# Two fused projection stages: the last SwiGLU part taken chunk by chunk, the first silu between the norm's steps, the first weight block in halves

## The reference, cut to what matters

```python
xp = xp + ab_out(...) @ w_out             # output projection and residual add
h = rmsnorm(x, norm_ffn[layer])
x = x + (silu(h @ w_gate) * (h @ w_up)) @ w_down      # D_FF = 2816
# layer 0 only, at the head of layer 1:
h = rmsnorm(x, norm_mix[1]);  z = h @ w_qkv           # 1024 x 3072
```

## Time and profile before

| | us |
|---|---|
| median of three runs | 3500.93 (3499.95 to 3503.22) |
| the profiled execution | 3503.33 |
| its span, first to last instruction | 3501.2 |
| PE busy in it | 3178.9 (91%) |
| trunk0, first load to last product | 903.2 to 2114.4 |
| trunk1, first load to last product | 2563.5 to 3471.7 |

### The profile page before, as it was taken

One profiled execution on the slowest core, in us unless ns is written; L12 is line 12 of the kernel. 1 busy time (PEld: TensorE's weight loads), 2 busy tenths in 40 slices (PEclk: granted clock), 3 DMA queues, 4 the chain that ended last, 5 costly groups with the idle time before them and its releaser, 6 DMA issues. The chain is left out here.

```text
span 3501.2 us, 48490 instructions
## 1 busy us (share of the span) xinstructions
PE 3178.9 (91%) x19094; PEld 3024.3 (86%) x19094; DVE 1108.2 (32%) x2190; ACT 846.2 (24%) x1606; POOL 993.7 (28%) x656
## 2 busy tenths in 40 slices
PE   6997558699889999999989996999978999999998
PEld 5997337588889999999989995777778999999997
DVE  3111672445131221112232113665623122112223
ACT  3001333355231111111131002444423111111111
POOL 3211102101352222223252213445435232222320
PEclk8998768799999999999999997999989999999998
DMA  3222514822211111111102225443421111111101
GB/s 107 99 92 75 141 48 142 86 58 62 73 49 37 36 60 48 36 36 60 36 25 74 95 73 128 91 95 82 84 73 48 37 36 60 48 36 36 60 12 58
DMA packets 201725, 230.20 MB, mean 66 GB/s; under 512 B 62400, under 2 KB 177297, under 8 KB 201377
## 3 DMA queue, kind: packets, MB, share of 16 engines
q1 hardware_dynamic: 201600, 228.51, 23.3%
HBM read 181.92 MB, written 54.44 MB: 68 GB/s over the span
## 5 line engine op out<-in xcount | busy, mean ns | idle before, releaser
L1101 PE MATMUL trunk_banks<-hhi,trunk_whi 128*128 128x384 f32 (+1 forms) x3072 | 1007.2, 328 | 58.6 <-POOL trunk_wlo L1044 34.3
L1103 PE MATMUL trunk_banks<-hhi,trunk_wlo 128*128 128x384 f32 (+1 forms) x3072 | 1004.5, 327 | 0.0
L1102 PE MATMUL trunk_banks<-hlo,trunk_whi 128*128 128x384 f32 (+1 forms) x3072 | 1004.5, 327 | 0.0
L1101 PEld LDWEIGHTS trunk_banks<-hhi,trunk_whi 128*128 128x128 f32 x3072 | 579.6, 189 | 60.4 <-POOL trunk_wlo L1044 34.7
L1102 PEld LDWEIGHTS trunk_banks<-hlo,trunk_whi 128*128 128x128 f32 x3072 | 579.6, 189 | 0.8
L1103 PEld LDWEIGHTS trunk_banks<-hhi,trunk_wlo 128*128 128x128 f32 x3072 | 579.5, 189 | 0.0
L1044 POOL TENSOR_TENSOR trunk_wlo<-trunk_stage,trunk_whi 128x2048 fp32r<-128x2048 f32 x86 | 395.7, 4614 | 552.8 <-ACT trunk_whi L980 552.8
L1171 DVE TENSOR_TENSOR trunk_act<-trunk_silu,trunk_banks 128x384 f32<-128x384 f32 x132 | 70.0, 532 | 970.5 <-PE trunk_banks L1103 947.4
L1178 DVE TENSOR_TENSOR xT<-xT,trunk_banks 128x384 f32<-128x384 f32 (+1 forms) x528 | 280.5, 532 | 235.5 <-PE trunk_banks L238 235.4
L1050 POOL TENSOR_TENSOR trunk_alo<-trunk_act,trunk_ahi 128x384 fp32r<-128x384 f32 x132 | 128.0, 970 | 793.8 <-ACT trunk_ahi L993 793.8
L236 PE MATMUL trunk_banks<-trunk_ahi,trunk_whi 128*128 128x384 f32 (+1 forms) x1056 | 346.3, 328 | 3.8 <-DVE xT L1178 3.8
(11 more groups left out here) (306 smaller groups left out, 4109.9 us busy)
## 6 DMA issues: line engine op xcount, KB each, us to landing
trunk_stage<-in_w_gate SPq DMA_DIRECT2D x22, 1024.0 KB
trunk_stage<-in_w_up SPq DMA_DIRECT2D x22, 1024.0 KB, 5.2
trunk_stage<-in_w_down SPq DMA_DIRECT2D x22, 1024.0 KB, 4.8
trunk_stage<-in_w_qkv SPq DMA_DIRECT2D x12, 1024.0 KB, 5.2
park_z<-in_rows SPq DMA_DIRECT2D x22, 544.0 KB
in_stage<-in_w_in SPq DMA_DIRECT2D x11, 1024.0 KB
park_z<-trunk_stage SPq DMA_DIRECT2D x48, 192.0 KB, 1.9
band_q_in<-park_z SPq DMA_DIRECT2D x32, 272.0 KB
```

Of the source, the lines that this page charges most:

```text
L1101: nc.tensor.matmul(out, tiles_of(m, whi)[:, f, k, :], hhi[:, k, c0:c0 + w], start=(k == 0), stop=False)
L1102: nc.tensor.matmul(out, tiles_of(m, whi)[:, f, k, :], hlo[:, k, c0:c0 + w], start=False, stop=False)
L1103: last = nc.tensor.matmul(out, tiles_of(m, wlo)[:, f, k, :], hhi[:, k, c0:c0 + w], start=False, stop=(k == KT - 1))
```

## The change

- **First block in halves.** The first `w_out` block is loaded as two DMAs of 512 KB, each into a contiguous half of 128 columns; ACT copies each half, and DVE instead of POOL subtracts it. The other blocks are as before.
- **First silu among the norm's steps.** ACT takes the silu of (c0, half 0) between `high` of c1 and `root` of c2, and that of (c0, half 1) behind `high` of c2; DVE's two products move along. The split of the first `w_down` block comes behind them, on ACT and on POOL.
- **Last part of trunk0 chunk by chunk.** PE does gate and up of c0 and c1, down of c0, gate and up of c2, down of c1, down of c2, then `w_qkv`. Down products rotate over three banks (4 to 6), bank 7 holds `means` and `roots` of the norm ahead, and its scratch `hf` moves to `stage[2]`; the `w_qkv` products use banks 0 to 3 and leave through `silu` and `act32`. The low parts of the first two `w_qkv` blocks are made on DVE (`low_of`), among the adds, instead of on POOL.

The diff, cut to its core (the rest splits functions by chunk without moving a step):

```diff
 # FlowNorm.total, with shared=True for the norm ahead
-        if c >= 2:
-            pe.wait_ge(self.eps_added, c - 1)
+        n = len(self.means)
+        if c >= n:
+            pe.wait_ge(*((self.scaled, KT * c) if self.shared else (self.eps_added, c - n + 1)))
...
 # SP
-            for u in range(3):
+            for h in range(2):
+                sp.dma_start(halves_of(stage[2])[:, h], columns(w_out)[:, :, h * P:(h + 1) * P]).then_inc(first_in[h], 16)
+            for u in (1, 2):
                 load_columns(A_SET[u], columns(w_out), u)
...
 # ACT
+            for h in range(2):
+                act.wait_ge(first_in[h], 16)
+                nc.scalar.activation(halves_of(whi[2])[:, h], halves_of(stage[2])[:, h], ACT.Copy).then_inc(first_hi, 1)
...
             norm.high(act, 1)
+            silu_of(0, 0, 0, first=True)
             norm.root(act, 2)
             norm.high(act, 2)
-            split(2, 2, a_sum, 24)
-            hidden(0, first=True)
+            silu_of(0, 0, 1, first=True)
+            for f in range(F):
+                high_of(0, 0, f)
+            split(2, 1, a_sum, 24)
+            for c in range(1, NC):
+                hidden(0, c)
...
+                for n in range(KT):
+                    ahead.square(act, n, added, O * LAST + n + 1)
+                silu_of(LAST, 2, 0)
+                ahead.root(act, 0)
+                ahead.high(act, 0)
+                silu_of(LAST, 2, 1)
...
 # POOL, last part
-                for u in range(2):
-                    split(u, 1 + parts)
-                for n in range(2 * KT):
+                for n in range(KT):
                     ahead.keep(pool, n)
                 ahead.low(pool, 0)
-                for n in range(2 * KT, O):
+                hidden(LAST, 2)
+                for n in range(KT, O):
                     ahead.keep(pool, n)
...
 # PE, last part
+                gate_up(LAST, 0)
+                gate_up(LAST, 1)
+                pe.wait_ge(w_lo[2], LAST + 2)
+                down_of(LAST, 0, last=True)
+                gate_up(LAST, 2)
+                down_of(LAST, 1, last=True)
+                down_of(LAST, 2, last=True)
...
 # DVE
+            def low_of(u):
+                dve.wait_ge(w_hi[u], 2 + parts)
+                nc.vector.tensor_tensor(wlo[u][:], stage[u][:], whi[u][:], ALU.subtract).then_inc(w_lo[u], 1)
```

More of the change, by code:

```diff
@@ L910, in trunk_stage @@
         stored = [st.sem(f"stored{r}") for r in range(BANKS)]
+        first_in = [st.sem(f"first_in{h}") for h in range(2)]
+        first_hi, first_lo = st.sem("first_hi"), st.sem("first_lo")
+        rows = [x[:, f, :] for x in (silu, act32) for f in range(F)]
         quarter = lambda tile, i: tile[:, i * W:(i + 1) * W]
@@ L1068, in _ @@
             norm.low(pool, 2)
-            split(2, 2)
-            hidden(0)
+            hidden(0, 0)
+            split(2, 1)
+            for c in range(1, NC):
+                hidden(0, c)
             with pool.Fori(1, LAST) as i:
@@ L1104, in product_of, with gate_up @@
                 return last
-            def part(i, first=False, last=False):
+            def gate_up(i, c, first=False):
+                w = CHUNKS[c][1]
+                for f in range(F):
+                    n = G * i + c * F + f
+                    if not (first and c == 0):
+                        pe.wait_ge(product, n - 1)
+                    for m, done in ((0, gate_sum), (1, up_sum)):
+                        if first and c == 0:
+                            pe.wait_ge(a_added, len(A_ORDER) - BANKS + 2 * f + m + 1)
+                        product_of(banks[:, 2 * f + m, 0:w], m, f, c, norm if first and f == m == 0 else None).then_inc(done, 1)
+                    if first and c == 0 and f == 0:
+                        norm.total(pe, 2)
+                    if i is LAST and ahead and c == 2 and f == 0:
+                        ahead.total(pe, 0)
@@ new lines, in down_of @@
+            def down_of(i, c, first=False, last=False):
+                c0, w = CHUNKS[c]
+                down = [t[2][:].rearrange("p (f k n) -> p k f n", f=F, k=KT) for t in (whi, wlo)]
+                pe.wait_ge(act_lo, G * i + (c + 1) * F)
+                for k in range(KT):
+                    d, b = c * KT + k, 4 + k % 4
+                    if last:
+                        b = 4 + d % 3
+                        pe.wait_ge(added, O * i + d - 2 if d >= 3 else O * i)
+                    elif not (first and d < BANKS):
+                        pe.wait_ge(added, O * i + d + 1 - BANKS)
+                    three_pass(nc, banks[:, b, 0:w], down[0][:, k], down[1][:, k], ahi, alo, F, c0, w).then_inc(out_sum, 1)
+                    if last and d == 2 * KT + 5:
+                        ahead.total(pe, 1)
@@ L1107, in part, with weights @@
+            def weights(i):
                 for m in range(2):
                     pe.wait_ge(w_lo[m], i + 2)
-                for c, (c0, w) in enumerate(CHUNKS):
-                    for f in range(F):
-                        n = G * i + c * F + f
-                        if not (first and c == 0):
-                            pe.wait_ge(product, n - 1)
-                        for m, done in ((0, gate_sum), (1, up_sum)):
-                            if first and c == 0:
-                                pe.wait_ge(a_added, len(A_ORDER) - BANKS + 2 * f + m + 1)
-                            product_of(banks[:, 2 * f + m, 0:w], m, f, c, norm if first and f == m == 0 else None).then_inc(done, 1)
-                        if first and c == 0 and f == 0:
-                            norm.total(pe, 2)
@@ L1120, in part @@
-                pe.wait_ge(w_lo[2], i + 3)
-                down = [t[2][:].rearrange("p (f k n) -> p k f n", f=F, k=KT) for t in (whi, wlo)]
-                for c, (c0, w) in enumerate(CHUNKS):
-                    pe.wait_ge(act_lo, G * i + (c + 1) * F)
-                    for k in range(KT):
-                        if not (first and c == 0 and k < BANKS):
-                            pe.wait_ge(added, O * i + c * KT + k + 1 - BANKS)
-                        three_pass(nc, banks[:, 4 + k % 4, 0:w], down[0][:, k], down[1][:, k], ahi, alo, F, c0, w).then_inc(out_sum, 1)
-                        if last and ahead and c and k == 3:
-                            ahead.total(pe, c - 1)
@@ L1202, in _ @@
             with dve.Fori(1, LAST) as i:
-                gated(i)
+                for c in range(NC):
+                    for f in range(F):
+                        gated(i, c, f)
                 for c in range(NC):
```

225 lines of the change are left out of this document (144 added, 81 removed).

## The result

The changed kernel takes 3453.49 us (median of four runs, 3447.62 to 3454.34) against 3502.07 before; the ratio is 0.985 with a 95% interval of 0.9824 to 0.9876. The forecast was 3452, so the time and all three terms of the sum came out near what was written. The profiled execution of the changed kernel took 3453.55, its span is 3451.8.

The account below looks back on a forecast made before the run. PE, busy 91% of the span, was taken as the bound, so its waits and slow stretches counted. Gains 10.8 + 29.4 + 9 = 49.2 from 3500.93 gave 3451.7, say 3452 us; range 3445 to 3461.

Parts of the forecast that it names:

- The halves: Head of both stages: first w_out block in halves cuts issue to first product to 7.0 us, gaining 10.8 in all.
- the bounds of 4.0 and 6.0: Head gain per stage: 4.0 us if the half lands at 5.84, 6.0 if it lands in 3.9 flat.
- Two signs that the prediction named: Head: a half load landing after 5 us or more meant wrong; heads the same in both stages meant right.
- The first silu: Part 0, both stages: moving the silu early removes the 12 us waits and slow stretches behind them, gaining 29.4 us.
- The page's rule against this edit: Part 0: 1283 ns table load plus some 1380 ns drain per change of set; some 2 us less gain.
- The end of trunk0: Last part of trunk0, chunk by chunk: new waits of 6.6 us against 16.8 lost before; gain taken as 9.
- the discount from 10.2 to 9: End of trunk0: gain lowered because the four short waits may cost some time at the lower clock level.
- the 16.8 of the sum: Old end of trunk0: time lost in 41.58 us, of which 12.0 idle and 4.8 at the lower level.
- the second silu was not late: Rival, part 0: scale and high of c2 drag over 2.4 us; 10 us less gain, 3462; chance 5%.
- no wait moved elsewhere: Rival: waits only move, to w_down or the second block; time stays near 3500; chance 2%.
- the clock stood at 1.00 through the 271 us: Rival, w_qkv phase: short waits bring the clock to 1.2 GHz and it stays; beyond 3590 us; chance 2%.
- The first rival: End of trunk0 gives nothing: waits grow from 6.6 to 16.8 us, total gain 40, time 3461; chance 7%.

Follow-up runs that it names:

- the added copies: Changed kernel with unused 2048-column copies ahead of ACT's second silu in part 0: two in trunk0, three in trunk1 (3460.17 us), or five and one (3458.89 us).
- the kernel with the end spaced out: Changed kernel with adds, low_of, second weight copy and emptying of first w_qkv banks reordered at the end of trunk0: 3447.35 us, ratio 0.9851 to before.

## Why the prediction was right

- **What bounds the kernel.** PE's waits and the stretches behind them were taken as the whole account, and they were: 49.9 us by the marks against 49.2 written. The waits in the two stages went from 70.5 to 30.1 us, and what was lost behind them at the lower level, by the granted clock, from 14.0 to 3.8: 40.4 and 10.2 less. Each of these marks is from one profile and scatters by about 1 us; means over all profiles that share a part give 9.8 for the heads, 28.6 for part 0 and 10.2 for the end, 48.6 in all.
- **The halves: 10.8 written, 10.2 measured** (9.5 in the run with the halves alone). In trunk0 the chain is 4.52 + 1.06 + 1.23 with 0.08 of handoffs, as written; copy and subtraction took the same in every profile with halves. The mis-sized term is the load: 4.5 us to ACT's copy was taken, and it was 5.71 in trunk1, so that the head gives 4.7 there, inside the bounds of 4.0 and 6.0. (With 7.0 for the new head, the 12.78 of the earlier trace rows would have given 5.8 in trunk1 and not the 5.4 of the sum.) That trunk0 came out as written is luck: over the sixteen heads with a half load in the runs it took 4.05 to 5.73 us, 5.1 in the mean, and only one was shorter than this 4.52. Two signs that the prediction named went against it here, a half load of 5 us or more and two heads that are not the same (they differ by 1.2). The mechanism stands, and the size of this term was off.
- **The first silu: 29.4 written, 30.2 measured** (29.6 alone). The steps came as written: `high` of c1 to the gated product 2.39 us (2.4), slack 5.1 (5.2) and 2.3 (2.4) by the trace, 2.6 by the added copies. The slow stretch behind the wait went with it. Of the 30.2, 1.0 is not the silu's: the stretch at the lower level behind the two heads, which this mark holds as well, happened to be that much shorter (0.67 to 0.74 and 0.54 to 0.63 over 6 us).
- **The page's rule against this edit.** The trace has 1.28 for the load, and a silu 1.30 and 1.29 us after its load began, in an order that now loads three times. The Trainium skill, page "ScalarE: Activation LUTs", section "What ACT_TABLE_LOAD costs", adds some 1380 ns of drain to each change of set; the trace does not agree, since no such time stands on either side of a load here, and two such drains, 2.8 us as an estimate from that page's figure, would have used up the slack of 2.3.
- **The end of trunk0: 9 written, 9.5 measured.** The four waits were priced at 2.8, 1.4, 1.4 and 1.0 and are 2.78, 1.22, 1.04 and 1.03, each where it was put. What did not hold is the discount from 10.2 to 9, for time at the lower level behind the short waits. The lower level did come behind the wait of 2.78 in five of eight profiles, but it cost nothing, since it only filled the waits that follow; that the first profile has 1.00 there is chance, as far as is known. The gain is still under 10.2 because the time lost before was a little less than the 16.8 of the sum. The windows behind the two waits of the kernel before show 4.4 of loss at the lower level, not 4.8 (six microseconds at 0.55 and six at 0.72):

```profile
1808.40:1814.40 6.00, 6.00 (x18) 5.39 (x19) 4.00 (x4) 3.71 (x6) 3.52 (x5) 0.55 0.00 0
...
1824.00:1830.00 6.00, 6.00 (x29) 6.00 (x30) 5.93 (x10) 2.65 (x7) 5.57 (x7) 0.72 0.02 4
```

  That leaves 16.4 less 6.1, 10.3, still 0.9 over what was measured. Some 0.4 of it is the price of the lower level: matmul instructions of 384 columns start 0.32 us apart there and 0.174 at 1.00 (second profile of the changed kernel), so a microsecond at the lower level loses 0.46 and not 0.5. The rest is open; in the two other profiles with the old end it took 1037.37 and 1037.51, so one profile is good to about 1 us here.
- **The rivals.** The end gave its share, the second silu was not late, no wait moved elsewhere, and the clock stood at 1.00 through the 271 us behind the short waits. The first rival was the one with something behind it: with the two subtractions left on POOL, the wait on `keep` comes back at 7.5.

## What to carry to other kernels

Where one engine is busy nine tenths of the time, write down its waits one by one with the chain behind each, and price an edit as the chain before minus the chain after, plus the slow stretch that goes with the wait. Where it came, that stretch cost 1.4 to 3.1 us here, whatever the length of the wait, and nothing where PE would have waited again right behind it. Edits on different waits added up here, 48.5 one by one against 49.9 together. Where a step is pulled forward in an engine's queue, price what it pushes back by its slack at the consumer, and measure that slack by adding known delays. When a chain at the end of a phase is short of room on two engines, look first at which queue holds the longest instruction ahead of the step that is waited for.

## What the runs showed of the hardware

- A wait of PE costs more than its length when the lower level follows, and the length alone does not tell whether it does. In the two stages of the thirteen traces, all 22 waits of 0.53 to 1.50 us left the granted clock at 1.00; of nine waits of 2.26 to 2.79, six brought the lower level; and all 40 of 3.29 us and more did. What was lost behind a wait (one less the granted clock, over the stretch at the lower level) was 1.4 to 3.1 us and did not grow with the wait: 3.1 behind 2.79, 1.6 behind 3.29, 2.8 behind 7.18, 1.5 behind 12.06. What decides it behind the 2.78 is open.
- Products that nobody uses, run in the wait, kept the clock up where they reached the first real product or nearly so: behind 0.87 us of standing still and behind none it was 1.00 in the first 6 us, behind 2.26 it was 0.72, behind 4.68 it was 0.56. The Trainium skill, page "TensorE: Matmul & The Clock Gate", section "Part 1: The HAM clock gate (the "warmup" mystery)", tells of two levels, set by how busy PE has been of late; the trace agrees in so far as all windows lie between 0.50 and 1.00. Behind the same wait of 2.78, it was not the same level from trace to trace.
- The same subtraction of 2048 columns on DVE took 2.29 us with POOL idle at its start and 2.71 where POOL was in the middle of its adds. In the kernel with the end spaced out it started first, and a copy on POOL that takes 0.50 elsewhere took 2.22 and ended 0.36 behind DVE's end at 1782.68 (timelines of DVE and POOL):

```profile
1780.39 2.29 DVE L1269 TENSOR_TENSOR trunk_wlo<-trunk_stage,trunk_whi 128x2048 fp32r<-128x2048 f32 x1
...
1780.82 2.22 POOL L816 COPY trunk_acc<-trunk_sq 128x384 f32<-128x384 f32 x1 [0.76 <-ACT trunk_sq L807]
```

  The Trainium skill, page "SBUF — State Buffer", section "SBUF: two separate sides", has the two engines share a port pair that whichever starts first holds for its whole instruction; the trace agrees in both directions, by 0.42 and by 1.7 us.
- The landing of the first load scatters more than its size explains. From issue to the first instruction that uses it, 256 KB took 2.76 and 3.00 us or 4.71 and 4.75 in two kernels, each kernel with one short and one long; 512 KB took 4.05 to 5.73 in sixteen cases, and 1 MB 5.12 to 6.75 in six. The list that gave 3.9 for `mla_V`'s loads of 512 KB has 4.1 for those of 256 KB.
